# All 62 taps of a causal convolution on VectorE instead of 40 there and 22 on GpSimd

## The reference

```python
def conv_group(a, g, conv_w, conv_b, ln_g, ln_b):
    u = a * jax.nn.sigmoid(g)
    y = lax.conv_general_dilated(
        u, conv_w[:, None, :].astype(u.dtype), window_strides=(1,),
        padding=[(CONV_WIDTH - 1, 0)], dimension_numbers=('NWC', 'WIO', 'NWC'),
        feature_group_count=CONV_CH) + conv_b
    y32 = y.astype(jnp.float32)
    mu = jnp.mean(y32, axis=-1, keepdims=True)
    var = jnp.mean(jnp.square(y32 - mu), axis=-1, keepdims=True)
    y32 = (y32 - mu) * lax.rsqrt(var + LN_EPS) * ln_g.astype(jnp.float32) + ln_b.astype(jnp.float32)
    return jax.nn.silu(y32).astype(a.dtype)

def hybrid_mixer(h, w_in, ...):
    p = h @ w_in
    ...
    o_gla = gla_group(...)
    o_conv = conv_group(ca, cg, conv_w, conv_b, conv_ln_g, conv_ln_b)
    o_swa = swa_group(sq, sk, sv, swa_sinks)
    return jnp.concatenate([o_gla, o_conv, o_swa], axis=-1) @ w_out
```

## Time and profile before

| | |
|---|---|
| median of three timed runs | 1591.98 us (1589.17 to 1592.87) |
| profiled execution, first to last instruction | 1590.1 us |
| TensorE (PE) busy | 97% |
| VectorE (DVE) busy | 70% |
| ScalarE (ACT) busy | 45% |
| GpSimd (POOL) busy | 11% |
| transfers | 252 MB, mean 159 GB/s |

### The profile page before, as it was taken

How to read it: one execution, slowest core, us unless ns; L and a number is a source line. 1 busy time by engine, 2 the same in 40 slices (tenths; PEclk the granted TensorE clock), 3 DMA queues, 4 the chain that set the end, 5 groups by cost and what they waited for, 6 DMA issues and landing times.

```text
span 1590.1 us, 31272 instructions
## 1 busy us (share of the span) xinstructions
PE 1535.1 (97%) x12682; PEld 1514.0 (95%) x12682; DVE 1110.1 (70%) x1446; ACT 720.8 (45%) x908; POOL 181.6 (11%) x191
## 2 busy tenths in 40 slices
PE   6999999999999999999789999999999987999998
PEld 5999999999999999999779999999999986999998
DVE  6766786677744766567977767567665699776654
ACT  4433853555533444434335544445443424454442
POOL 0000000000001000012904000010000264300000
PEclk8999999999999999999879999999999997999999
DMA  8544455566555566555116665656655540556661
GB/s 267 195 133 133 159 188 184 155 178 179 181 179 159 148 180 181 192 159 125 62 59 154 181 181 183 195 135 185 185 187 170 133 133 1 160 160 182 180 195 51
DMA packets 378774, 252.28 MB, mean 159 GB/s; under 512 B 24371, under 2 KB 377924, under 8 KB 378692
## 3 DMA queue, kind: packets, MB, share of 16 engines
q1 hardware_dynamic: 377808, 248.54, 53.0%
q10 hardware_dynamic: 884, 2.58, 0.5%
HBM read 250.04 MB, written 1.05 MB: 158 GB/s over the span
## 4 chain that ended last, share of the span: by engine, by line
PE 83%; DVE 13%; ACT 2%; issue 1%; DMA 1%; SPq 0%; ACTq 0%; DVEq 0%
PE stream L1429 57%; PE psm L1429 23%; DVE w_lo L789 3%; DVE yc L1246 3%; PE ps L1429 3%; ACT w_hi L480 2%; DVE s_gla L1258 1%; DMA raw<-in_w_in 1%; DVE x L867 1%; DVE hn L857 1%; DVE a_lo L835 0%; DVE ss L1273 0%; DVE sq L1330 0%; DVE pt L879 0%; DVE yc L1243 0%
## 5 line engine op out<-in xcount | busy, mean ns | idle before, releaser
L1429 PE MATMUL stream<-a_hi,w_hi 128*128 128x256 f32 x2464 | 707.6, 287 | 12.4 <-DVE a_lo L820 9.1
L1429 PE MATMUL stream<-a_lo,w_hi 128*128 128x256 f32 x2464 | 701.2, 285 | 0.0
L1429 PE MATMUL stream<-a_hi,w_lo 128*128 128x256 f32 x2464 | 700.9, 284 | 0.0
L789 DVE TENSOR_TENSOR w_lo<-raw,w_hi 128x2048 fp32r<-128x2048 f32 x240 | 552.5, 2303 | 175.7 <-ACT w_hi L480 175.6
L480 ACT ACTIVATE w_hi<-raw 128x2048 fp32r<-128x2048 f32 x240 | 457.1, 1907 | 235.9 <-PE psm L1429 153.7
L1429 PEld LDWEIGHTS stream<-a_hi,w_hi 128*128 128x128 f32 x2464 | 476.6, 193 | 18.5 <-issue 9.8
L1429 PEld LDWEIGHTS stream<-a_lo,w_hi 128*128 128x128 f32 x2464 | 477.1, 194 | 0.0
L1429 PEld LDWEIGHTS stream<-a_hi,w_lo 128*128 128x128 f32 x2464 | 476.9, 194 | 0.0
L1429 PE MATMUL psm<-h_hi,w_hi 128*128 128x256 f32 x896 | 251.7, 281 | 0.0
L1429 PE MATMUL psm<-h_lo,w_hi 128*128 128x256 f32 x896 | 251.7, 281 | 0.0
L1429 PE MATMUL psm<-h_hi,w_lo 128*128 128x256 f32 x896 | 251.7, 281 | 0.0
(11 more groups left out here) (246 smaller groups left out, 1525.4 us busy)
## 6 DMA issues: line engine op xcount, KB each, us to landing
raw<-in_ffn_w_up SPq DMA_DIRECT2D x136, 512.0 KB, 5.1
raw<-in_ffn_w_down SPq DMA_DIRECT2D x104, 512.0 KB, 3.7
raw<-in_ffn_w_gate SPq DMA_DIRECT2D x88, 512.0 KB, 4.0
raw<-in_w_in SPq DMA_DIRECT2D x80, 512.0 KB, 4.6
raw<-in_w_out SPq DMA_DIRECT2D x24, 512.0 KB, 4.0
raw<-in_w_in SPq DMA_DIRECT2D x20, 256.0 KB, 4.6
raw<-in_w_ret_o SPq DMA_DIRECT2D x8, 512.0 KB, 4.0
raw<-in_w_lru_o SPq DMA_DIRECT2D x8, 512.0 KB, 4.3
```

The source lines that it names most:

```text
L789: V.tensor_tensor(w_lo[s][:, :, :], raw[s][:, :, :], w_hi[s][:, :, :].bitcast(F32), ALU.subtract).then_inc(w_split, 1)
L1429: return nc.tensor.matmul(dst, lhs, rhs, start=start, stop=stop, skip_group_check=True)
```

## The change

The constant `TAPS_DVE`, the two GpSimd tiles, the 43 GpSimd operations per layer and their two semaphores are taken out. The list of steps on VectorE has all 62, in the order tap by tap, half 0 and then half 1; the calls of `conv` ahead of the last keep their counts (3, 3, 2, 6 and sixteen times 1). The addition of GpSimd's sum goes.

```diff
-TAPS_DVE = 9
...
-        y_pool, y_tap = hn[:, 4, :], hn[:, 5:7, :]
...
-        up_ready, tap_product, tap_sum, ss_ready, ss_exp, p_ready = (sem(n) for n in (
-            "up_ready", "tap_product", "tap_sum", "ss_ready", "ss_exp", "p_ready"))
+        up_ready, ss_ready, ss_exp, p_ready = (sem(n) for n in ("up_ready", "ss_ready", "ss_exp", "p_ready"))
...
-                pool.wait_ge(up_ready, l + 1)
-                products, sums = (TAPS - TAPS_DVE) * l, (TAPS - TAPS_DVE - 1) * l
-                for n in range(TAPS - TAPS_DVE):
-                    tap = TAPS_DVE + n
-                    at = VL["conv_w"] + 2 * tap + 1
-                    dst = y_tap[:, n % 2, :] if n else y_pool
-                    if n > 2:
-                        pool.wait_ge(tap_sum, sums + n - 2)
-                    nc.gpsimd.tensor_tensor(dst, up[:, 1, tap:tap + T], vecs[:, 2 + l, at:at + 1].broadcast_to([P, T]),
-                                            ALU.mult).then_inc(tap_product, 1)
-                    if n:
-                        pool.wait_ge(tap_product, products + n + 1)
-                        if n > 1:
-                            pool.wait_ge(tap_sum, sums + n - 1)
-                        nc.gpsimd.tensor_tensor(y_pool, y_pool, dst, ALU.add).then_inc(tap_sum, 1)
...
-                conv_steps = [(tap, f) for tap in range(TAPS) for f in range(2) if f == 0 or tap < TAPS_DVE]
+                conv_steps = [(tap, f) for tap in range(TAPS) for f in range(2)]
...
                 conv(len(conv_steps))
-                dve.wait_ge(dve_chain, conv_at[TAPS - 1, 0])
-                dve.wait_ge(tap_sum, (TAPS - TAPS_DVE - 1) * (l + 1))
-                V.tensor_tensor(yc[0][:, 1, :], yc[0][:, 1, :], y_pool, ALU.add)
+                dve.wait_ge(dve_chain, conv_at[TAPS - 1, 1])
                 link(V.tensor_tensor(yc[0][:, 0, :], yc[0][:, 0, :], yc[1][:, 0, :], ALU.add))
                 V.tensor_tensor(yc[0][:, 1, :], yc[0][:, 1, :], yc[1][:, 1, :], ALU.add).then_inc(yc_ready, 1)
```

## The result

The changed kernel takes 1598.38 us (median of five runs, 1597.71 to 1601.27) where the kernel before, run beside it, takes 1592.87 (1589.17 to 1593.77). The ratio is 1.0044, with a 95% interval of 1.0031 to 1.0056: slower by 5.5 us by the medians and by 7 by the ratio. The forecast was 1595.3 us and +0.21%; the sign is right, and the forecast is about half of what the ratio gives (0.6 of the difference of the medians).

What follows compares the result with a forecast made beforehand. TensorE bounds most of the span, VectorE the convolution stretch of each mixer. Two layers at +0.5 us plus 2.3 us for TensorE's clock make +3.3 on the median 1591.98: 1595.3 us, range 1592.0 to 1599.5.

Steps and rivals of the forecast that it cites:

- What bounds the kernel: TensorE over most of the span; in each mixer's convolution stretch VectorE, about 755 to 811 us in the first layer.
- What is given back: VectorE's steps beside GpSimd's taps return to their undisturbed price, 8.2 us a layer off its path.
- What is added: 22 more steps in VectorE's tail, 8.7 us a layer, less 0.4 for the dropped addition of GpSimd's sum.
- The new waits: VectorE, getting ahead, waits for TensorE at the second window scores: 0.4 us a layer, bounds 0 and 0.8.
- the first wait: VectorE ahead of the second window scores: they come about 0.8 us late if TensorE's clock falls, otherwise nothing is lost.
- the second wait: VectorE ahead of the fifth score evacuation, TensorE late at low clock: up to 2.7 us a layer; chance 0.16.
- The clock behind the tail: After a nine-us pause TensorE restarts at 1.2 GHz behind the convolved rows; newly paid in layer two, 2.3 us, bounds 0 to 4.6.
- The first rival: No new clock cost, since the kernel before already restarts slowly in both layers in some executions: 1593.0 us, chance 0.20.
- the TensorE rival: TensorE at low clock becomes the bound in the score part, 3.0 us more: +6.3 us, 1598.3 us, chance 0.16.
- the two large terms: Per layer on VectorE, 8.2 us given back against 8.7 added less 0.4: net +0.1 us.
- Faster: Stalls beside GpSimd's two key products also go, gain capped at 2.5 us a layer: 1588.0 us, chance 0.06.
- No relief: VectorE's doubled steps have another cause that stays, so 8.2 us are not returned: +19.7 us, 1611.7 us, chance 0.04.

Runs made afterwards that it cites:

- `no_taps`: The kernel before with GpSimd's 22 taps of half 1 and the addition of their sum left out: ratio 0.993, 1580.3 us.
- `both`: The changed kernel with GpSimd's taps put back beside VectorE's 62 steps, their sum unused: ratio 1.0132, 1612.62 us.
- `warm_tail`: The changed kernel with 44 idle TensorE products in each layer's long pause before the convolved rows: ratio 1.0042, 1597.37 us.
- `best_b`: As `late_free_warm`, with 14 idle products before the second window scores and 2 and 3 steps moved into VectorE's later waits: ratio 0.9974, 1587.72 us.
- `best_a`: As `late_free_warm`, with 9 steps moved from the tail into VectorE's waits and 40 idle products in the pause: ratio 0.9994, 1590.37 us.
- `late_free_warm`: From the kernel before: GpSimd takes only the last 12 taps, after the second window-score copies; 44 idle TensorE products in the pause: ratio 1.0006, 1593.46 us.

## Why the prediction was right and where it was wrong

**What bounds the kernel: right.** Only VectorE's part and the way behind moved; everything behind the first gate input and outside these two took the same time.

**What is given back: right.** 8.2 us was the sum; 8.1 is what `no_taps` gave in the layer without waits. The single lines came out as well, but for one: 2.35 for the 128x1024 pair (2.28 was assumed), 0.87 for two steps (0.88), 2.44 for six (2.46). The first pair was too hopeful, 3.38 to 3.02, 0.36 instead of 0.6.

**What is added: right.** 8.3 us was the sum; `both` gave 8.4 to 8.6. Where no wait fell (the first layer of `warm_tail`), VectorE's part is 63.74 us, 0.4 more than before; +0.1 was the net.

**The new waits: the step that failed.** The prediction named the place of the first wait, its cause and its price correctly: 0.8 us if the clock falls (0.6 to 0.9 was measured). It took 0.4 a layer and 0.9 at most for everything, and put the second wait, ahead of the fifth scores, among the rivals at a chance of 0.16, so the sum had it at nothing. Its argument against was that TensorE's pauses there get shorter. They do: 1.15 us is left of 1.95 in front of the fourth scores in the first layer (not shown), and yet the clock was low in that part in all six layers of the three executions. It had been low there in the kernel before as well, 0.50 from 785.20 to 792.00 and from 1321.10 to 1327.90, in the trace that the prediction was made from; the argument from shorter pauses passed over that. So the rival is what happened, beside the forecast: in each of those layers 0.7 or 2.1 to 2.3 us. The term of the waits was 2.2 us a layer in the mean instead of 0.4. The rival's price for the second wait was 1.5 us with half of the products slow, and its measured mean is 1.4.

**The clock behind the tail: right in kind, too large.** The long pause (9.4 us, nine were expected) and the mean products at 2.04 us in both layers were as forecast. But the price was read from one execution, as 12.50 - 10.20 of its two layers, and the 13.11 us of its first layer are the longest of the six before. In six layers each it costs 12.53 - 11.69 = 0.84 a layer, 1.7 us in all, instead of 2.3. The first rival (the kernel before pays already in some layers) was partly true: it paid in three of six.

**The sum.** By the means of the three executions of each kernel: 2 x (65.97 - 63.39) = 5.2 in VectorE's part, 1.7 behind it, together 6.8 us; the spans of those executions are 1596.8 and 1589.8 us in the mean, 7.0 apart. The forecast had 1.0 and 2.3. The range reached to 1599.5 and held the time, for it took in the TensorE rival; the point did not. The rival's own time, 1598.3, is the median measured (1598.38), and that is in part luck: it had 3.8 us of waits, 0.2 for the two large terms and 2.3 for the clock, where 4.4, 0.7 and 1.7 were measured. The forecast's own range, 1593.7 to 1597.1, does not follow from its bounds of +2.5 and +4.1 us, which give 1594.5 to 1596.1, and the bounds 0 and 4.6 of the clock term are in neither.

**The other rivals.** "Faster" needed the stalls beside the key products to go: the step before the pair (a `tensor_scalar`) still takes 2.50 us and the pair 3.02, beside the key products. "No relief" is ruled out by `no_taps`.

## What to carry to other kernels

Work moved from VectorE to GpSimd is not free because GpSimd is off the path: compare the duration of the same VectorE instruction beside GpSimd's work and without it, and multiply by the number of such instructions. Here 22 taps cost VectorE 8.1 us by their mere running and 8.7 us when it does them itself, so neither division wins; taps placed beside VectorE's PSUM readers do, with VectorE's own steps in its waits and TensorE's clock held up by idle products (`best_b`; with the clock left low at the second window scores, `best_a` showed no gain that can be told). Where an engine is relieved by several microseconds, price the waits that the relief uncovers, at the low as well as at the high clock of TensorE, before netting two large terms to nothing.

## What the runs showed of the hardware that was not expected

GpSimd's fills, 90 in 33.24 us, do not slow VectorE's two-input steps at all, while its additions and products double their pitch from 0.40 to 0.83 us. Some operations with one SBUF input are held too: a 128x16 `tensor_scalar` took 0.72 instead of 0.17 us beside the taps of `late_free_warm`, and in every kernel here a 128x256 one took 2.50 us beside the key products where the one ahead of them took 0.35. No run takes the key products away, so this cause is read from the timelines alone.

TensorE's clock fell though it was busy for much of the time. In the first layer of the first profile of after, the granted clock fell to 0.50 at 768.73 us, behind a pause of 2.33, and again at 782.38, behind one of 1.15; that these pauses are the cause is not shown. Where it fell differed from execution to execution of one kernel, and the same instructions then cost VectorE 0, 0.7 or 2.2 us of waiting. A difference between two layers in one trace is not a difference between layers.
